# Attention heads in pairs with normalised weights, three expert tiles beside the ring, and one wait moved in a two-block transformer kernel

## The chip, the cores and the metric

The kernel runs on one core of one Trainium2 chip, as one program without a host in between. The metric is the device time of one execution in microseconds (us). The engines are called TensorE (PE in the rows; PEld is its weight load), VectorE (DVE), ScalarE (ACT), GpSimd (POOL) and SyncE (SP). SyncE here only issues transfers.

## What is computed

All numbers are 32-bit floats; the model width is 1024 and the sequence 256 rows. A first block of two layers works on the stream and on 256 context rows; a second block of two layers works on the first one's result and on 256 memory rows.

First block, per layer:

```python
hx = x * (1 + sc1) + sh1                     # modulation from c @ w_ada
q, k, v, cb, cc, cv, gu, gv = split(hx @ w_in)
att = window_attention(q, k, v, k_ctx, v_ctx, sink)    # 8 heads of 64, 2 key heads
o = concat([att, local_mixers(cb, cc, cv, gu, gv)]) @ w_out
x = layer_norm(ALPHA * x + g1 * o)
x = layer_norm(ALPHA * x + g2 * hier_moe(x * (1 + sc2) + sh2))   # 32 experts, top 2
```

In layer 0 the context rows go the same way, in layer 1 they give keys and values alone. Second block, per layer:

```python
ya = sliding_window_attention(rope(q_a), rope(k_a), v_a, sinks) * silu(g_a)   # 8 heads of 64
yb = forgetting_attention(q_b, k_b, v_b, log_sigmoid(f_b)) * silu(g_b)        # 8 heads of 64
yc = rms_norm(state_space_part * silu(z))
x = x + concat([ya, yb, yc]) @ w_out
x = x + memory_cross_attention(rms_norm(x), rms_norm(mem))                    # 4 heads of 256
```

In each of the attentions the weights of a row are p / (sum(p) + exp(sink - m)) with p = exp(s - m), where s are the masked scores and m their largest; those without a sink leave its term out.

## The kernel before

**Order.** Each engine has its program written out by hand, and they wait for each other by semaphores. The stages follow each other: layer 0 of the first block (projections, attention, mixing product, routing, experts), layer 1 the same, then the second block's layers.

**Ring.** All large weights come through a ring of four tiles of 2 MB. SyncE issues them in the order of use (`dense`, line 1278): for tile g it first waits until tile g - 4 is released, which the table `released` says as a semaphore and a count. The experts have three tiles each (w1, w3, w2), 96 in a layer, and TensorE takes them in that order from the ring; in a layer of 32 experts the first eleven tiles are written out and the rest run in loops (line 1315). The modulation weights (`ada`, line 584) pass through the ring too, and their products stand as filling work beside the attention.

**Attention.** A unit is one head of one tile of 128 query rows. `attention` exists three times, for TensorE (line 522), ScalarE (1524) and VectorE (1884). Per unit TensorE makes the scores (lines 568, 1120), VectorE adds mask and, in the forgetting attention, the sums of the gates, takes the row's maximum (1925) and writes its negative; ScalarE makes the exp with the row's sum beside it (1529); TensorE transposes the weights in blocks of 128 keys (507), ScalarE copies them out (1516), and TensorE weighs the values (541): the turned weights, 128x128, are the stationary operand, the values, 128x64, the moving one. Eight heads of a query tile share one bank. When they are done, VectorE asks ScalarE for the exp of the sinks, adds, takes the reciprocals and multiplies the bank by them (1899, 1833). The rows so attended are later transposed by TensorE and copied by ScalarE, since the product that follows wants the features on the partitions.

TensorE takes two units in turn; beside each unit a `fill` runs: products of the other projections, gate rows or modulation tiles in the first block, stream products in the second (1051 where the result is turned, 1037 where it is rows). VectorE takes the fills' results in `beside_first`, `beside_last`, `beside_a`, `beside_b`, ScalarE serves gelu, square root and other functions between its units, each with a change of its table. In layer 0 of the first block the products are fills 0 to 16 without every third, and the tiles of modulation rows 4 to 8 stand at fills 2, 5, 8, 11 and 14, rows 9 to 11 at 19, 21 and 23, and those of the next layer at 25, 27, 29 and 31. The tile of product weights that is released last, `cx_at`, is in use up to fill 16.

**Experts.** Tokens are gathered in blocks by GpSimd (line 1431) into `hb`, four blocks at a time, turned by TensorE (832), and each expert's three products run in 64-column halves side by side (866).

**Memory rows.** The second block's keys and values of the memory are made beside the first block. The last of them is written to `kv_scratch` by ScalarE's queue after the second layer's experts. VectorE waits for that transfer (`kv_out`, line 2548) ahead of the second block, since the buffer `hb` is written again there. The second block's first rows are taken in a loop over two row tiles (2655 to 2667).

```python
            def weigh(i):
                n, h = units[i]
...
                for k in range(nkc(n)):
                    last = mm(T["bank"][:, o:o + hw], sbuf_pT[:, i % 2, k, :], values(n, h, k),
                              start=(k == 0), stop=(k == nkc(n) - 1))
```

## Time and profile before

| | us |
|---|---|
| runs | 2308.99, 2307.2, 2302.45 |
| median | 2307.2 |
| the profiled execution | 2304.22 |
| its span, first to last instruction | 2302.4 |

The mean granted clock of TensorE in the profiled execution is 0.985. A row of the timeline gives start, duration, engine, line, operation, output and inputs, sizes, how many instructions are merged, and in brackets the idle time before it with what ended it. Durations of TensorE overlap their followers a little, since its ends are modelled. Busy shares are averages over stages with different limits, so the rows below are taken stage by stage.

### The profile page before, as it was taken

What the parts mean: (1) busy time and instruction counts of PE and PEld (TensorE: products, weight loads), DVE (VectorE), ACT (ScalarE), POOL (GpSimd) and SP (SyncE); (2) the same over time, 40 slices, a digit from 0 to 9 for tenths busy, and PEclk for the clock granted to TensorE, in tenths of its full rate; (3) what the DMA queues carried; (4) which work ended last, traced back from release to release, by engine and by line L of the source; (5) the groups of instructions that cost most, each with busy time, mean ns of one, the idle gap of its engine ahead of it and who ended that gap; (6) DMA issues with size and microseconds to landing.
All of it is one profiled execution on the core that took longest, in us unless ns stands there. A gap on an engine that the chain in (4) does not pass through costs nothing.

```text
span 2302.4 us, 30476 instructions
## 1 busy us (share of the span) xinstructions
PE 2035.6 (88%) x11971; PEld 1212.3 (53%) x11972; DVE 786.6 (34%) x1836; ACT 457.2 (20%) x1059; POOL 189.7 (8%) x240
## 2 busy tenths in 40 slices
PE   6999999799877789999877777798999999999998
PEld 4566566444433335757433333344875575775574
DVE  1355674111111116656111111114466312456413
ACT  2142112111111112411111111111123212123112
POOL 1000001111111110001111111111000000000000
PEclk9999999999999999999999999999999999999999
DMA  9235649999999985686999999996343332343230
GB/s 376 110 129 240 255 156 378 423 426 427 427 425 426 425 345 211 236 317 257 424 425 425 424 425 425 427 420 242 134 182 129 111 147 110 147 165 129 95 142 19
DMA packets 62872, 640.95 MB, mean 278 GB/s; under 512 B 15868, under 2 KB 16420, under 8 KB 24240
## 3 DMA queue, kind: packets, MB, share of 16 engines
q1 hardware_dynamic: 41728, 588.39, 61.9%
q0 software_dynamic: 19984, 44.74, 5.5%
q10 hardware_dynamic: 1056, 6.37, 0.7%
q8 instruction: 73, 1.20, 0.2%
q14 instruction: 31, 0.25, 0.0%
HBM read 622.50 MB, written 44.17 MB: 290 GB/s over the span
## 4 chain that ended last, share of the span: by engine, by line
PE 62%; DMA 31%; DVE 4%; ACT 2%; issue 1%; SPq 0%; POOL 0%; DVEq 0%
DMA ring<-in_moe 26%; PE ps L866 10%; PE ps L1037 10%; PE ps L519 8%; PE ps L1051 6%; PE ps L1148 5%; PE ps L507 3%; PE ps L695 3%; DMA ring<-in_denseA 3%; PE ps L1220 2%; PE ps L872 2%; PE ps L1016 2%; PE ps L541 2%; PE ps L771 2%; PE ps L584 1%; DMA ring<-in_denseB 1%
## 5 line engine op out<-in xcount | busy, mean ns | idle before, releaser
L866 PE MATMUL ps<-ring,scr 128*64 128x256 f32 (+1 forms) x4800 | 667.5, 430 | 178.2 <-DMA ring<-in_moe 169.3
L866 PEld LDWEIGHTS ps<-ring,scr 128*64 128x64 f32 x4800 | 333.4, 138 | 485.9 <-DMA ring<-in_moe 239.3
L1833 DVE TENSOR_TENSOR scr<-ps,scr 128x512 f32<-128x512 f32 (+3 forms) x98 | 54.6, 558 | 574.6 <-PE ps L866 487.0
L1037 PE MATMUL ps<-ring,hT 128*128 128x512 f32 (+1 forms) x576 | 245.5, 578 | 5.1 <-ACT hT L1546 5.1
L519 PE MATMUL ps<-ring,hT 128*128 128x512 f32 (+1 forms) x512 | 199.3, 547 | 0.5 <-ACT hT L1516 0.5
L1444 POOL DMA_INDIRECT ys_scratch<-scr,ytab x128 | 125.0, 976 | 825.4 <-DVE scr L2495 791.6
L1670 ACT ACTIVATE scr<-ps 128x512 f32<-128x512 f32 x64 | 38.2, 597 | 760.8 <-PE ps L866 694.0
L2495 DVE COPY scr<-ps 128x1024 f32<-128x1024 f32 x64 | 78.4, 1224 | 269.3 <-PE ps L866 243.4
L1037 PEld LDWEIGHTS ps<-ring,hT 128*128 128x128 f32 x576 | 108.1, 193 | 117.8 <-issue 108.2
L1516 ACT ACTIVATE scr<-ps 128x256 f32<-128x256 f32 (+2 forms) x168 | 71.3, 436 | 403.7 <-PE ps L507 403.7
L519 PEld LDWEIGHTS ps<-ring,hT 128*128 128x128 f32 x512 | 97.3, 193 | 93.0 <-issue 89.2
L1051 PE MATMUL ps<-hT,ring 128*128 128x256 f32 x640 | 145.5, 382 | 0.0
L1051 PEld LDWEIGHTS ps<-hT,ring 128*128 128x128 f32 x640 | 118.8, 190 | 17.4 <-issue 0.7
L1529 ACT ACTIVATE scr<-scr,small 128x256 f32<-128x256 f32 (+2 forms) x128 | 67.6, 528 | 50.0 <-DVE small L1837 40.9
L584 PE MATMUL ps<-ring,small 128*32 128x128 f32 x1536 | 55.9, 307 | 22.8 <-DMA ring<-in_denseA 22.8
L541 PEld LDWEIGHTS ps<-scr 128*128 128x128 f32 x512 | 66.0, 194 | 16.5 <-issue 15.3
L507 PE MATMUL ps<-cst,scr 128*128 128x128 f32 x332 | 61.1, 281 | 13.9 <-ACT scr L1529 11.6
L541 PE MATMUL ps<-scr 128*128 128x64 f32 x512 | 65.5, 274 | 2.7 <-DVE hb L1833 2.7
L695 PE MATMUL ps<-hT,ring 128*128 128x512 f32 (+1 forms) x192 | 65.6, 490 | 0.0
L584 PEld LDWEIGHTS ps<-ring,small 128*32 128x32 f32 x1536 | 47.7, 123 | 33.0 <-issue 16.4
L1833 DVE TENSOR_TENSOR scr<-ps,cst 128x256 f32<-128x256 f32 (+2 forms) x96 | 32.7, 341 | 85.5 <-PE ps L568 74.3
L872 PE MATMUL ps<-ring,scr 128*128 128x512 f32 x128 | 57.1, 599 | 5.0 <-DMA ring<-in_moe 5.0
(330 smaller groups left out, 2019.2 us busy)
## 6 DMA issues: line engine op xcount, KB each, us to landing
ring<-in_moe SPq DMA_DIRECT2D x192, 2048.0 KB, 15.9
ring<-in_denseB SPq DMA_DIRECT2D x48, 2048.0 KB, 7.7
ring<-in_denseA SPq DMA_DIRECT2D x36, 2048.0 KB, 16.2
scr<-ys_scratch POOLq DMA_DIRECT2D x6, 1024.0 KB, 7.2
modB<-mod_scratch POOLq DMA_DIRECT2D x10, 512.0 KB, 11.3
ring<-kv_scratch SPq DMA_DIRECT2D x2, 2048.0 KB, 8.6
tok_scratch<-hb POOLq DMA_DIRECT2D x6, 512.0 KB, 2.9
memT_scratch<-modB ACTq DMA_DIRECT2D x2, 1024.0 KB, 6.7
```

The lines of the kernel that those rows point to most:

```text
L507: last = nc.tensor.transpose(bank[:, i * P:(i + 1) * P], c, ident)
L519: last = mm(bank[:, 0:cols], lhs(c), w(c), start=(c == 0), stop=(c == n - 1))
L541: last = mm(T["bank"][:, o:o + hw], sbuf_pT[:, i % 2, k, :], values(n, h, k), start=(k == 0), stop=(k == nkc(n) - 1))
L584: last = mm(bank[32 * q:32 * q + 32, 0:P], cact32[:, c, :], w[:, c, q * P:(q + 1) * P], start=(c == 0), stop=(c == DC - 1))
L695: last = mm(T["open"][:, 0:tok], w[:, c, off:off + P], hT8[:, c, 0:tok], start=(c == 0), stop=(c == DC - 1))
L866: last = mm(out, lhs(c)[:, 0:64], w(c)[:, half * q:half * (q + 1)], start=(c == 0), stop=(c == n - 1))
L872: last = mm(ps[:, bank, :], lhs(c), w(c), start=(c == 0), stop=(c == n - 1))
L1037: last = mm(T["open"][:, 0:cols], hT16[:, c, t * P:(t + 1) * P], w[:, c, 0:cols], start=(c == 0), stop=(c == DC - 1))
L1051: last = mm(T["open"][:, q * 256:(q + 1) * 256], w[:, c, m * P:(m + 1) * P], hT16[:, c, :], start=(c == 0), stop=(c == DC - 1))
L1148: last = mm(bank, lhs(c), w[:, c, :], start=(c == 0), stop=(c == DC - 1))
L1444: pool.indirect_dma_start(halves, bass.IndirectOffsetOnAxis(ap=ytab[:, h, b:b + 1], axis=0), y[:, h * 512:(h + 1) * 512], None, bounds_che ...
L1833: return V.tensor_tensor(out, a, b, op)
```

## The change

**Pairs.** The five attentions with heads of 64 run as `paired_attention`; the memory attention keeps the old way under its own name. Units go two and two. The sink is one more column of the scores, so the row's sum holds it. VectorE takes the reciprocal per unit, ScalarE multiplies the weights by it, then they are transposed. In the weighing the values are stationary and the turned weights of 128 rows moving; the two heads of a pair use the two halves of the columns, so the result has its features on the partitions. The transpositions of the attended rows and their copies go; the gate streams `ga` and `gb` are made in turned form. The fills get new places.

**Tiles beside the ring.** In layer 1 the expert tiles at places 3, 7 and 10 of the order are loaded to buffers that are free there, in two halves each, and not through the ring; SyncE issues the first after the last query and key tiles are turned, the other two after the second expert tile. Blocks of tokens have two buffers there, where they had four.

**Wait.** VectorE's wait for `kv_out` moves from the end of the second layer's experts to the second row tile of the second block's first layer.

```diff
+ASIDE = ((), (3, 7, 10))
+
+BLOCK_BUFFERS = (4, 2)
...
-TURNED = ("x0", "x1", "x2", "qb", "kb")
+TURNED = ("x0", "x1", "x2", "qb", "kb", "ga", "gb")
...
+    own_beside = ((2, 5, 8, 11, 14, 16, 17, 19), (4, 6, 8, 9, 10, 11, 12, 13))
+    next_beside, product_beside = (22, 25, 28, 31), (0, 1, 2, 3, 5, 7)
...
+        def paired_attention(units, score, values, nkc, fill):
...
+            for i in range(0, len(units), 2):
+                n, h = units[i]
+                for k in (i, i + 1):
+                    need("scaled", p_scaled)
+                    turn_weights(k, nkc(n))
+                    turned = T["tp"]
+                    if k == i:
+                        for at in range(i + 2, min(i + 4, len(units))):
+                            score(*units[at])
+                    if k > 0:
+                        fill(k)
+                if h == 0:
+                    T["bank"] = av_bank()
+                pe.wait_ge(tp_free, turned)
+                for b in range(nkc(n)):
+                    for q in range(2):
+                        last = mm(T["bank"][HD * q:HD * q + HD, h // 2 * P:(h // 2 + 1) * P], values(n, h + q, b),
+                                  sbuf_pT[:, q, b, :], start=(b == 0), stop=(b == nkc(n) - 1))
...
-            for t in range(nt):
-                need("h", h_ready)
-                turn([hb[:, t, i * P:(i + 1) * P] for i in range(4)])
+            need("h", h_ready, nt)
...
-            for t in range(NX):
-                need("h", h_ready)
-                for c in (0, 4):
-                    turn([mixB[:, t, (c + i) * P:(c + i + 1) * P] for i in range(4)])
+            need("h", h_ready)
+            out_attended(0, 0)
+            need("h", h_ready)
...
+            if l > 0:
+                sp_.wait_ge(*free_when["turned", l])
+                load_aside(0)
+            expert_tile(0)
+            expert_tile(1)
+            if l > 0:
+                sp_.wait_ge(*free_when["routed", l])
+                sp_.wait_ge(rows_out, 16 * 9)
+                load_aside(1)
+                load_aside(2)
...
+        def paired_attention(units, nkc, sink, serve, after=None):
+
+            for i in range(0, len(units), 2):
+                for k in (i, i + 1):
+                    n, h = units[k]
+                    weights(k, n, h, P * nkc(n) + sink)
+                for k in (i, i + 1):
+                    n, h = units[k]
+                    p = sbuf_p[:, k % 2, 0:P * nkc(n)]
+                    T["inv"] += 1
+                    act.wait_ge(inv_ready, T["inv"])
+                    A(p, p, ACT.Copy, scale=rinv[:, n, h:h + 1]).then_inc(p_scaled, 1)
+                for k in (i, i + 1):
+                    copy_turned(sbuf_pT[:, k % 2, 0:nkc(units[k][0]), :], nkc(units[k][0]))
+                    if after:
+                        after(k)
+                if i > 0:
+                    serve(i - 1)
+                serve(i)
+            serve(len(units) - 1)
...
+            for i in range(0, len(units), 2):
+                for k in (i, i + 1):
+                    scores(k)
+                if i == 0 and opening:
+                    opening()
+                for k in (i, i + 1):
+                    inverse(k)
+                if i > 0:
+                    extra(i - 1)
+                extra(i)
+                if i > 0 and units[i][1] == 0:
+                    finish(units[i][0] - 1, av_job())
...
-                dve.wait_ge(kv_out, 16 * 2 * DEPTH)
...
+                if l == 0 and t == 1:
+
+                    dve.wait_ge(kv_out, 16 * 2 * DEPTH)
```

## Rows read from the trace of the kernel before

**Rows 1.** The page: busy time and share of each engine; the chain that ended last.

```profile
PE 2035.6 (88%) x11971; PEld 1212.3 (53%) x11972; DVE 786.6 (34%) x1836; ACT 457.2 (20%) x1059; POOL 189.7 (8%) x240
...
PE 62%; DMA 31%; DVE 4%; ACT 2%; issue 1%; SPq 0%; POOL 0%; DVEq 0%
DMA ring<-in_moe 26%; PE ps L866 10%; PE ps L1037 10%; PE ps L519 8%; PE ps L1051 6%; PE ps L1148 5%; PE ps L507 3%; PE ps L695 3%; DMA ring<-in_denseA 3%; PE ps L1220 2%; PE ps L872 2%; PE ps L1016 2%; PE ps L541 2%; PE ps L771 2%; PE ps L584 1%; DMA ring<-in_denseB 1%
```

**Rows 2.** Stretches: length, busy time per engine, clock, DMA share, GB/s.

```profile
1040.00:1080.00 40.00, 36.24 (x200) 30.06 (x199) 26.32 (x109) 7.13 (x13) 4.92 (x6) 0.96 0.55 194
1080.00:1160.00 80.00, 65.48 (x505) 35.23 (x506) 16.78 (x36) 14.77 (x30) 11.56 (x13) 1.00 1.01 425
...
1730.00:1750.00 20.00, 20.00 (x74) 10.48 (x72) 19.02 (x52) 5.28 (x15) 0.00 (x0) 1.00 0.27 105
1600.00:1610.00 10.00, 8.21 (x21) 5.68 (x22) 6.44 (x22) 2.98 (x10) 0.00 (x0) 0.66 0.11 23
```

**Rows 3.** TensorE in order of time, first block's attention, four key chunks.

```profile
122.27 1.90 PE L541 MATMUL ps<-scr 128*128 128x64 f32 x16
...
125.59 1.95 PE L584 MATMUL ps<-ring,small 128*32 128x128 f32 x64
```

**Rows 4.** TensorE in order of time, second block's forgetting attention: one chunk, two chunks.

```profile
1722.87 0.55 PE L541 MATMUL ps<-scr 128*128 128x64 f32 x4
...
1739.72 1.00 PE L541 MATMUL ps<-scr 128*128 128x64 f32 x8
```

**Rows 5.** TensorE in order of time, second layer's experts.

```profile
1093.11 1.09 PE L832 MATMUL ps<-cst,hb 128*128 128x128 f32 x8
1094.13 3.65 PE L866 MATMUL ps<-ring,scr 128*64 128x512 f32 x16
...
1111.30 3.67 PE L866 MATMUL ps<-ring,scr 128*64 128x256 f32 x32 [1.32 <-DMA ring<-in_moe]
```

**Rows 6.** ScalarE in order of time, first block's attention: copy, exp.

```profile
133.78 0.60 ACT L1516 ACTIVATE scr<-ps 128x512 f32<-128x512 f32 x1 [4.31 <-PE ps L507]
134.27 0.71 ACT L1529 ACTIVATE scr<-scr,small 128x512 f32<-128x512 f32 x1
```

**Rows 7.** Line 1529: its table loads, ns shortest/median/longest, first and last start.

```profile
L1529 ACT ACT_TABLE_LOAD  x10: 1283/1283/1283, 111.7 to 2238.1; - x10
```

**Rows 8.** TensorE in order of time, end of layer 0's attention.

```profile
203.60 3.64 PE L584 MATMUL ps<-ring,small 128*32 128x128 f32 x64 [1.89 <-DMA ring<-in_denseA]
...
240.17 1.73 PE L541 MATMUL ps<-scr 128*128 128x64 f32 x8
...
247.25 2.31 PE L519 MATMUL ps<-ring,hT 128*128 128x512 f32 x5
```

**Rows 9.** SyncE's queue in order of time, 194 to 212 us.

```profile
195.91 11.72 SPq L1278 DMA_DIRECT2D ring<-in_denseA  x5
```

**Rows 10.** VectorE in order of time: layer 1's first norm; start of the second block.

```profile
1017.32 1.23 DVE L1841 SCALAR_TENSOR_TENSOR hb<-modB,scr 128x1024 f32<-128x1024 f32 x1 [4.57 <-DMA scr<-in_ln_b]
...
1599.16 0.09 DVE L2654 MEMSET scr<- 128x36 f32 x1 [11.52 <-DMA kv_scratch<-hb]
```

**Rows 11.** TensorE in order of time, start of the second block.

```profile
1585.01 3.94 PE L1037 MATMUL ps<-ring,hT 128*128 128x280 f32 x16
...
1589.66 7.03 PE L1037 MATMUL ps<-ring,hT 128*128 128x512 f32 x16
1601.79 13.39 PE L1037 MATMUL ps<-ring,hT 128*128 128x280 f32 x32 [5.10 <-ACT hT L1546]
```

**Rows 12.** TensorE in order of time: between the second block's attentions, and their end.

```profile
1701.61 0.49 PE L1120 MATMUL ps<-scr 64*128 64x128 f32 x2 [0.43 <-DVE scr L1841]
1702.97 0.33 PE L507 MATMUL ps<-cst,scr 128*128 128x128 f32 x1 [0.87 <-ACT scr L1529]
...
1784.52 1.04 PE L507 MATMUL ps<-cst,hb 128*128 128x128 f32 x8
...
1787.70 2.84 PE L1148 MATMUL ps<-ring,scr 128*128 128x512 f32 x6 [0.74 <-ACT scr L1516]
```

446 lines of the change are left out of this document (230 added, 216 removed).

## The prediction

> **What bounds the kernel now.** I read the page's shares and its chain first [rows 1]: TensorE is busy for 88% of the span and holds 62% of the chain that ended last, DMA 31%, and 26% of the span is expert weights arriving in the ring. VectorE and ScalarE together hold 6%. So two prices are paid: TensorE work in the dense stages, and bytes in the expert stages. The stretches show it [rows 2]: from 1080 to 1160 us the queues move 425 GB/s at a full DMA share and TensorE is busy 65.48 of 80 us, waiting for tiles as at 1111.30 [rows 5]; from 1040 to 1080, ahead of the second layer's experts, they move only 194; from 1730 to 1750, in the second block's attention, TensorE is busy all 20 us and VectorE 19.02 of them. An edit that shortens TensorE work counts in the last kind of stretch, one that takes bytes out of the ring in the first, and in the attention the next engine to be late is VectorE.
>
> **Part 1: the pairs.** Five attentions run 56 pairs of units: 8 of four key chunks and 8 of two in the first block's layer 0, 8 of four in layer 1, and per layer of the second block 8 of one chunk and 8 of two.
>
> *Weighing.* A four-chunk pair holds 1.90 us of TensorE (16 records) [rows 3], a two-chunk pair 1.00 and a one-chunk pair 0.55 [rows 4]. After the change the values stand still in 64 columns, and two heads stream 128 columns each into the two halves. The trace has that form at other widths: an expert product of 32 records in 128x64 halves, 256 columns each, takes 3.67 us [rows 5], so 16 records of 128 columns are 3.67/4 = 0.92; a modulation product, 64 records of 128 columns in four groups, takes 1.95 [rows 3], so 16 in two groups are 1.95 x 16/64 x 2 = 0.98. I take half of the old time less the overlapped ends: a gain of about 0.8, 0.35 and 0.15 us per pair. The other bound is the old durations, no gain.
>
> The rows show no price for changing the form: a 128x128 transposition of 1.09 us starts at 1093.11 and the 128x64 product at 1094.13, before the first one's modelled end [rows 5]. The Trainium skill (TensorEngine Tiling (Array Packing), Tiling Modes) says that a change of tiling mode drains the engine, and TensorE: Matmul & The Clock Gate puts a drain at some 175 ns. By that, two changes for each of 56 pairs would give back 112 x 0.175 = 19.6 us, an estimate from those pages; the row speaks against it, since it has no gap between the modes.
>
> *The longer chain.* Before, a unit went exp, transposition, copy, weighing, and the division came later, eight heads at once. Now exp (0.71 for 512 columns [rows 6]) is followed by VectorE's reciprocal and by a ScalarE scaling, as large as a copy (0.60 [rows 6]), before TensorE may transpose. Scores run one pair ahead, so this hides behind two fills where those are products of some 3.6 us; it shows where a fill is missing or something else sits in ScalarE's order. The sink column costs VectorE a short copy per unit, and the two reciprocals wait for exps that follow the pair's second score work. Queued behind them on VectorE are the takes of the fills.
>
> *Second block, per layer.* In the window attention 4 one-chunk pairs x 0.15 + 4 two-chunk x 0.35 = 2.0 us, on TensorE's path. Between it and the forgetting attention TensorE stood still for 0.43 + 0.87 us [rows 12]; the closing of the first now comes behind the opening of the second, so I count 1.3. The forgetting attention would give 2.0 again, but VectorE is at 95% there [rows 2]: with two reciprocals and a wait for the second exp, about 1 us per pair by the exp's duration, its pairs outlast TensorE's for three or four pairs, and I count 1.3. The 16 transpositions of the attended rows ended the stage: from 1784.52 to the output product at 1787.70, 3.2 us [rows 12], go. The turned gate streams cost about 0.2 (estimate, two short transposed products for two of rows). Sum 2.0 + 1.3 + 1.3 + 3.2 - 0.2 = 7.6 per layer, **-15.2 us** for both. Bounds: -6, if only the transpositions stay gained, to -22.
>
> *Layer 0 of the first block.* The first eight pairs gain 8 x 0.8 = 6.4. Against that the first pair waits for its whole chain, some 2.2 (two exps and a scaling, rows 6), and the gelu's and the square root's table changes, 1.28 there and 1.28 back each [rows 7], now stand in front of a pair's scalings with one product to cover them: some 4.5. So the last product ends where it did, +0.3. There its tile comes free, SyncE's next issues follow at 195.91 [rows 9], and the tile behind them is used at 203.60 [rows 8]. Before, that was in fill 19 of 31; now it is fill 16, and everything later stands behind the same landing. From there to the end of weighing (240.17 + 1.73) lay 38.3 us [rows 8] for 6.5 pairs, (38.3 - 3.6)/6.5 = 5.3 each without the first product; one more pair lies behind it now: +5.3. The 6.5 others gain 0.35 each and pay about 0.8 each for a scaling and two hand-overs that their short fills do not hide: +2.9. The attended rows' transpositions go: from the last weighing to the mixing product at 247.25 lie 5.3 us [rows 8], of which about 1 stays: -4.3. Sum 0.3 + 5.3 + 2.9 - 4.3 = **+4 us**. Bounds -2 (the chain hides as well as before) to +8.
>
> *Layer 1 of the first block.* The same 6.4, and half of the transpositions, 2.1, less about 5.5 for the start, the gelu and the square root, would bring the mixing product 3 us earlier. But what follows does not hang on TensorE alone: VectorE waits for `scr<-in_ln_b` until 1017.32, 4.57 us idle [rows 10], a transfer that POOL issues behind its modulation rows, and the extra expert tile that is loaded in this attention competes with it. I take **+1 us**, from -3 (those transfers move forward too) to +4.
>
> **Part 2: three tiles beside the ring.** A tile is 2.097 MB and at 425 GB/s [rows 2] takes 4.93 us. Three less in the ring's stream are 14.8 us, if they are loaded in time that is free: the 40 us before run at 194 GB/s [rows 2], which leaves 40 x 231 GB/s = 9.2 MB, more than 6.3. What it adds: SyncE waits at two places ahead of later tiles, none of which had a free slot there, and on POOL's queue the last two of four gathers of tokens wait for the first two blocks to be turned, with the loads of the closing norm behind them. The third block is wanted only at 1093.11 [rows 5], more than 10 us after. Behind an aside tile no slot comes free, so the queues may run empty for up to 2 us: **-13 us**, bounds -6 (TensorE's starting pace is the limit) to -15.
>
> **Part 3: the moved wait.** VectorE stands 11.52 us for `kv_scratch<-hb` until 1599.16 [rows 10], ahead of the first norm. TensorE stands 5.10 us and from 1601.79 runs 32 records in 13.39 us, where the same records took 3.94 + 7.03 = 10.97 just before [rows 11]; the granted clock in 1600 to 1610 is 0.66 [rows 2], between the levels of 1.2 and 2.4 GHz. With the wait at the second row tile, TensorE goes on from 1596.7 with those 32 records, which cover the landing. If the standstill goes, so do 5.10 + 2.42 = **-7.5 us**. Bounds -5 to -8: the products behind those records need VectorE's second tile, and each us by which the landing outlasts them costs one.
>
> **Sum.** -15.2 + 4 + 1 - 13 - 7.5 = -30.7 us on the profiled execution's 2304.2: 2273.5. The median of the runs shown, 2307.2, stands 3.0 above it, so I predict **2276 us**.
>
> **Rivals.** (a) The second block's pairs wait for VectorE throughout: for it speak the 19.02 of 20 us, against it that the convolution's work, which fills VectorE there, stands beside 8 of the forgetting attention's 16 units and 4 of the window attention's. The gain falls from 15.2 to about 2: 2289. (b) The tiles beside the ring give 5 us, as slots come free at TensorE's pace: 2284. (c) Weighing in halves keeps its old duration, by a drain or because the halves do not overlap: 6.4 + 2.8 + 6.4 + 4 x 2.0 = 24 us lost, 2300; rows 5 speak against it. (d) Slower: the first block's 24 pairs each show their chain of exp, reciprocal and scaling ahead of the transposition. At 2 us more per pair (two exps and a scaling, rows 6) that is 48: 2324. It decides from 30.7/24 = 1.28 us per pair. Against it: the products that stand beside most pairs. (e) The first block's stands hide after all and its pairs keep their gain, 13 us more: 2263. The change does what it says as far as the diff shows.
>
> **Chances.** Forecast 0.55, (a) 0.13, (b) 0.10, (c) 0.04, (d) 0.08, (e) 0.10. A measurement of this kernel can tell about 0.3%, 7 us, from no change. Faster by more: the forecast, (a), (b) and (e) less their bad ends, 0.86; within it those ends and (c), 0.06; slower (d), 0.08. The range 2257 to 2298 takes in (a), (b), (e) and the bounds of the costs together, and leaves out (c) and (d).
>
> **What would show it.** Right: weighing of a four-chunk pair under 1.1 us; no transpositions between the last weighing and the output products; the second expert stage shorter by about 13 us; no stand of TensorE near 1600. Wrong: TensorE waiting for ScalarE or VectorE in every pair of the second block; idle queues between 1080 and 1130; a mixing product of layer 0 over 10 us later.

## The result and the profile after

The changed kernel takes 2293.98 us (median of 7 runs, 2291.82 to 2297.82) against 2307.2 (2302.45 to 2311.1) for the kernel before, measured beside it: a ratio of 0.9947 with an interval of 0.9936 to 0.9958. That is 13.2 us faster where 31 were forecast; the time lies inside the range given, the gain at 42% of its size. In the profiled executions the spans are 2292.2 and 2302.4 us, 10.2 apart.

The page of the kernel after, its busy times and its chain, answers to [rows 1]:

```profile
PE 2013.8 (88%) x12043; PEld 1196.0 (52%) x12044; DVE 796.0 (35%) x1984; ACT 500.6 (22%) x1147; POOL 189.7 (8%) x240
...
PE 56%; DMA 29%; DVE 9%; ACT 3%; issue 1%; SPq 0%; POOL 0%; DVEq 0%
```

TensorE has 22 us less to do, and the span gains less than half of that. On the chain TensorE and DMA shrink, and VectorE goes from 4 to 9% and ScalarE from 2 to 3%: new waits stand where work was taken out.

To see where, I cut the span at the start of TensorE's first row of each stage (first score product, first mixing product, first expert product, first product of the memory's keys and values, first window score of the second block, first state-space product). The stretches between, in us; the runs e1 to e12 are told below:

| stretch | before | after | e1 | e2 | e3 | e8 | e10 | e12 |
|---|---|---|---|---|---|---|---|---|
| layer 0: attention to mixing | 135.5 | 146.7 | 136.8 | 150.5 | 135.4 | 136.2 | 136.1 | 135.2 |
| layer 0: mixing to experts | 108.8 | 110.4 | 110.5 | 110.0 | 111.9 | 108.5 | 112.7 | 111.8 |
| layer 1: attention to experts | 153.6 | 156.7 | 157.0 | 152.6 | 156.1 | 154.7 | 152.9 | 154.5 |
| layer 1: experts | 479.5 | 469.3 | 468.5 | 480.5 | 469.0 | - | 472.4 | 469.8 |
| memory rows to second block's first scores | 70.5 | 62.9 | 67.2 | 62.9 | 63.0 | 63.0 | 62.9 | 62.6 |
| second block, layer 0: both attentions and output product | 169.3 | 164.9 | 165.0 | 165.0 | 165.0 | 163.0 | 164.9 | 165.0 |
| the same, layer 1 | 169.3 | 165.0 | 165.4 | 165.1 | 165.7 | 163.0 | 165.2 | 165.2 |

After against before: layer 0's attention +11.2 and the 0.3 by which it begins later, its mixing product +1.6, layer 1 +3.1, experts -10.2, moved wait -7.6, second block -4.4 and -4.3; the sum is the span's -10.2 (to 0.1, the rounding). Every term of the forecast moved its way, but layer 0's attention loses 11 us where 4 were counted, and the second block gives 8.7 where 15.2 were. The mixing product of layer 0 starts 11.5 us later (258.75 against 247.25), which the prediction had named as a sign of being wrong.

**Layer 0's attention.** TensorE in order of time, kernel after, answering to [rows 8]:

```profile
205.20 3.23 PE L619 MATMUL ps<-ring,small 128*32 128x128 f32 x64 [7.61 <-DMA ring<-in_denseA]
...
224.47 0.44 PE L531 MATMUL ps<-cst,scr 128*128 128x128 f32 x2 [2.58 <-ACT scr L1604]
...
253.61 0.66 PE L574 MATMUL ps<-scr 128*64 128x128 f32 x8
256.19 0.63 PE L531 MATMUL ps<-cst,hb 128*128 128x128 f32 x4 [1.93 <-DVE small L2328]
```

The last product ends and releases its tile, and TensorE stands 7.61 us for the modulation tile that now follows at once. All eight two-chunk pairs are weighed behind it. Two more such stands follow (1.29 and 1.96 us), and between 220 and 252 TensorE stands nine times for ScalarE's copies (line 1578) and scalings (line 1604), 8.0 us in all.

**Weighing.** The first window attention of the second block, a pair of one chunk. First the kernel after (fill, weighing, transposition, scores), further down a pair of two chunks (with the transposition ahead of its fill) and, from the first block, one of four:

```profile
1628.58 3.62 PE L1091 MATMUL ps<-hT,ring 128*128 128x256 f32 x16
1632.13 0.44 PE L574 MATMUL ps<-scr 128*64 128x128 f32 x4
1632.50 0.33 PE L531 MATMUL ps<-cst,scr 128*128 128x128 f32 x1
1632.75 0.49 PE L603 MATMUL ps<-scr 64*128 64x128 f32 x4
...
1672.52 0.38 PE L531 MATMUL ps<-cst,scr 128*128 128x128 f32 x2
...
1676.27 0.66 PE L574 MATMUL ps<-scr 128*64 128x128 f32 x8
1676.86 0.44 PE L531 MATMUL ps<-cst,scr 128*128 128x128 f32 x2
...
144.91 1.09 PE L574 MATMUL ps<-scr 128*64 128x128 f32 x16
145.93 0.66 PE L531 MATMUL ps<-cst,scr 128*128 128x128 f32 x4
```

The same of the kernel before:

```profile
1630.51 3.62 PE L1051 MATMUL ps<-hT,ring 128*128 128x256 f32 x16
1633.96 0.55 PE L541 MATMUL ps<-scr 128*128 128x64 f32 x4
1634.35 0.28 PE L507 MATMUL ps<-cst,scr 128*128 128x128 f32 x1
1634.56 0.51 PE L568 MATMUL ps<-scr 64*128 64x128 f32 x4
...
1678.10 1.00 PE L541 MATMUL ps<-scr 128*128 128x64 f32 x8
1678.94 0.39 PE L507 MATMUL ps<-cst,scr 128*128 128x128 f32 x2
...
122.27 1.90 PE L541 MATMUL ps<-scr 128*128 128x64 f32 x16
124.00 0.60 PE L507 MATMUL ps<-cst,scr 128*128 128x128 f32 x4
```

Read from start to start, not by the durations. Weighing: four chunks 1.73 before, 1.02 after; two chunks 0.84 and 0.59; one chunk 0.39 and 0.37. And the neighbours grow: the same fill ahead of the weighing takes 3.45 before and 3.55 after, the transposition behind it 0.21 and 0.25. So a one-chunk pair loses 0.12 us, a two-chunk pair gains 0.11 and a four-chunk pair, if its neighbours grow as much, 0.6.

**The end of that stage.** Kernel after, answering to the last of [rows 12]: stream products run straight into the output product, and no transposition of attended rows stands between.

```profile
1775.44 6.60 PE L1077 MATMUL ps<-ring,hT 128*128 128x512 f32 x15
1781.88 7.03 PE L1189 MATMUL ps<-ring,hb 128*128 128x512 f32 x16
```

**The experts of layer 1.** The queues during that stage: the total, then the ring's queue and GpSimd's. Kernel before (1075.3 to 1554.9 us):

```profile
DMA packets 18990, 203.36 MB, mean 424 GB/s; under 512 B 5881, under 2 KB 5881, under 8 KB 6635
...
q1 hardware_dynamic: 13590, 198.01, 97.5%
q0 software_dynamic: 5242, 4.11, 2.6%
```

Kernel after (1091.7 to 1561):

```profile
DMA packets 18832, 198.07 MB, mean 422 GB/s; under 512 B 5854, under 2 KB 5854, under 8 KB 6864
...
q1 hardware_dynamic: 13156, 191.70, 96.8%
q0 software_dynamic: 5520, 5.16, 3.2%
```

The ring brings 6.3 MB less, which is three tiles. But GpSimd's queue brings 1.05 MB more inside the stage: with two block buffers in place of four, two of the four gathers come later, when the queues are full. GpSimd in the kernel before (the last of the four) and in the kernel after (the third; the fourth follows at 1098.32):

```profile
1062.38 0.94 POOL L1431 DMA_INDIRECT hb<-tok_scratch,slot_tok  x1 [0.30 <-issue]
```

```profile
1090.74 0.93 POOL L1493 DMA_INDIRECT hb<-tok_scratch,slot_tok  x1 [13.40 <-PE ps L865]
```

The stage saves 5.29 MB, not 6.29. It also begins less evenly: a stretch of the kernel after ahead of it (columns as in [rows 2]):

```profile
1080.00:1091.00 11.00, 9.57 (x48) 8.01 (x46) 4.97 (x21) 2.07 (x5) 0.26 (x1) 1.00 0.24 63
```

The queues run at 63 GB/s there; then the stage's first 32 records, at 1091.66, take 5.36 us at a granted clock of 0.68, where they take 3.67 at the full clock [rows 5].

**Layer 1's first norm.** VectorE in the kernel after, answering to the first of [rows 10], where it stood 4.57 us for the same transfer and the row began 16.5 us earlier:

```profile
1033.81 1.22 DVE L1916 SCALAR_TENSOR_TENSOR scr<-modB,scr 128x1024 f32<-128x1024 f32 x1 [9.41 <-DMA scr<-in_ln_b]
```

The attention begins 13.25 us later here, so 3.2 us are lost inside this layer; VectorE waits longer, for a transfer.

**The moved wait.** TensorE in the kernel after, answering to [rows 11]: no stand between 1591 and 1613.

```profile
1591.33 3.94 PE L1077 MATMUL ps<-ring,hT 128*128 128x280 f32 x16
1595.10 1.04 PE L531 MATMUL ps<-cst,S 128*128 128x128 f32 x8
1595.97 17.67 PE L1077 MATMUL ps<-ring,hT 128*128 128x512 f32 x48
```

### The profile page after: what moved, and what is told of

Same layout as the page of the kernel before. It is cut to its first block, busy times and chain, and to the rows that moved or that the text cites. A ratio compares the mean times of both kernels' runs of the same rounds, so it can differ in the third digit from the quotient of the medians.

```text
span 2292.2 us, 30890 instructions
## 1 busy us (share of the span) xinstructions
PE 2013.8 (88%) x12043; PEld 1196.0 (52%) x12044; DVE 796.0 (35%) x1984; ACT 500.6 (22%) x1147; POOL 189.7 (8%) x240
## 4 chain that ended last, share of the span: by engine, by line
PE 56%; DMA 29%; DVE 9%; ACT 3%; issue 1%; SPq 0%; POOL 0%; DVEq 0%
DMA ring<-in_moe 25%; PE ps L899 11%; PE ps L543 8%; PE ps L1077 8%; PE ps L1091 5%; PE ps L1189 5%; PE ps L531 3%; PE ps L1259 2%; PE ps L905 2%; PE ps L1056 2%; PE ps L803 2%; DVE scr L1908 2%; DMA ring<-in_denseA 2%; DVE scr L1916 1%; DMA ring<-in_denseB 1%; PE ps L731 1%
## 5 line engine op out<-in xcount | busy, mean ns | idle before, releaser
L899 PE MATMUL ps<-ring,scr 128*64 128x256 f32 (+1 forms) x4736 | 653.6, 428 | 172.5 <-DMA ring<-in_moe 163.9
L899 PEld LDWEIGHTS ps<-ring,scr 128*64 128x64 f32 x4736 | 328.4, 138 | 472.2 <-DMA ring<-in_moe 229.3
L1091 PE MATMUL ps<-hT,ring 128*128 128x256 f32 x896 | 204.1, 382 | 0.0
L1077 PE MATMUL ps<-ring,hT 128*128 128x512 f32 (+1 forms) x448 | 184.6, 566 | 0.0
L1091 PEld LDWEIGHTS ps<-hT,ring 128*128 128x128 f32 x896 | 166.2, 190 | 26.0 <-issue 3.3
L543 PE MATMUL ps<-ring,hT 128*128 128x512 f32 (+1 forms) x416 | 157.2, 531 | 0.2 <-issue 0.2
L1077 PEld LDWEIGHTS ps<-ring,hT 128*128 128x128 f32 x448 | 83.5, 190 | 85.6 <-issue 82.8
L543 PEld LDWEIGHTS ps<-ring,hT 128*128 128x128 f32 x416 | 78.6, 191 | 70.3 <-issue 67.3
L1590 ACT ACTIVATE scr<-scr,small 128x513 f32<-128x513 f32 (+4 forms) x128 | 67.8, 531 | 70.8 <-DVE small L1912 48.6
L531 PEld LDWEIGHTS ps<-cst,scr 128*128 128x128 f32 x332 | 38.2, 142 | 60.4 <-ACT scr L1604 29.7
L803 PE MATMUL ps<-scr,ring 128*128 128x256 f32 x256 | 64.7, 415 | 0.0
L1967 DVE TENSOR_REDUCE small<-scr 128x1 f32<-128x256 f32 (+2 forms) x128 | 58.0, 453 | 6.8 <-DVE scr L1908 0.3
```

Source lines behind the costliest of these rows:

```text
L531: last = nc.tensor.transpose(bank[:, i * P:(i + 1) * P], c, ident)
L543: last = mm(bank[:, 0:cols], lhs(c), w(c), start=(c == 0), stop=(c == n - 1))
L803: last = mm(T["open"][:, q * 256:(q + 1) * 256], w[:, c, m * P:(m + 1) * P], memT[:, c, :], start=(c == 0), stop=(c == DC - 1))
L899: last = mm(out, lhs(c)[:, 0:64], w(c)[:, half * q:half * (q + 1)], start=(c == 0), stop=(c == n - 1))
L1077: last = mm(T["open"][:, 0:cols], hT16[:, c, t * P:(t + 1) * P], w[:, c, 0:cols], start=(c == 0), stop=(c == DC - 1))
L1091: last = mm(T["open"][:, q * 256:(q + 1) * 256], w[:, c, m * P:(m + 1) * P], hT16[:, c, :], start=(c == 0), stop=(c == DC - 1))
```

## The experiments

Each run changes the kernel after unless it says otherwise. Ratios are to the kernel before on the same chip, whose medians lay between 2304.1 and 2305.9 us. Executions of one kernel spread over 3 to 10 us here, and a stage may differ by 3 to 4 us between two kernels with the same code in it: layer 1 below, and layer 0's attention, which takes 146.7 us in the kernel after, 150.5 in e2 and 151.1 in e7, with granted clocks of 0.83, 0.74 and 0.74 from 225 to 245 us. Smaller differences are read only where a stage is steadier: the experts of layer 1 take 467.5 to 469.3 us in the eight traces with three tiles beside the ring, the second block 164.9 to 165.7 per layer wherever its code is that of the change.

**e1: the first block with the old attention.** TensorE's, ScalarE's and VectorE's parts of the first block, its fills and its closing as before; the second block, the tiles and the wait as after.

```diff
-            paired_attention([(n, h) for n in range(nt) for h in range(NH)],
+            attention([(n, h) for n in range(nt) for h in range(NH)],
...
-                    if i in own_beside[0]:
-                        ada(own_at[4 + own_beside[0].index(i)])
...
+                    elif i in (19, 21, 23):
+                        ada(own_at[9 + (i - 19) // 2])
```

> The first block's two attentions go back to their old form (heads normalised at the end, rows turned afterwards, modulation tiles at fills 19, 21, 23 and 25 to 31); second block, tiles beside the ring and the moved wait stay as changed. Theory 1 (the first block's pairs are what gives the gain back): the mixing product of layer 0 starts again near 247 us (258.75 in the changed kernel, 247.25 before), layer 0's experts near 356 (369.20), and the total falls by 13.2 us for layer 0 and by up to 3 for layer 1's start of the experts: 2278 to 2281 us. Rival (the loss lies in what else changed in the first block: the residual's buffer, the tiles beside the ring, their transfers): layer 0's experts stay within 3 us of 369 and the total within 4 us of 2294.

Measured: 2286.74 us, ratio 0.9917 (0.9903 to 0.9932), so 7 faster than the kernel after, between the two theories. Layer 0's attention is back at 136.8. The pairs of the first block, as the change places them, cost time. The other theory's time is missed in part because the stretch ahead of the second block takes 67.2 us in this trace and not 62.9; e4 below shows why.

**e2: no tiles beside the ring, four block buffers.**

```diff
-ASIDE = ((), (3, 7, 10))
-BLOCK_BUFFERS = (4, 2)
+ASIDE = ((), ())
+BLOCK_BUFFERS = (4, 4)
```

> The changed kernel with all 96 expert tiles of layer 1 in the ring again and four buffers for the gathered blocks. Theory: the second expert stage is longer by the 10.3 us that it lost (79.5 us per 16 tiles as before), and the first of its products starts as late after the mixing product as in the changed kernel (77.0 us; 73.3 before), because VectorE's modulation rows come later, not because the tiles' transfers compete: total 2304. Rival (the first extra tile's transfer delays the modulation rows and the norm's parameters): the distance from mixing product to first expert product returns to 73.3 us, total 2301.

Measured: 2303.71 us, ratio 0.9996 (0.9985 to 1.0008): 10 us slower than after, and the experts' stage back at 480.5. The first expert product comes 72.5 us after the mixing product, the rival's distance (73.3) and not the theory's (77.0); but e7, with the tiles and the same code, has 75.0, so this does not decide whether the tiles' transfers compete. The tiles give 10 to 11 us, and without them the whole rest of the change, moved wait included, comes out at no change.

**e3: layer 0's modulation tiles at the fills of the kernel before.**

```diff
-    own_beside = ((2, 5, 8, 11, 14, 16, 17, 19), (4, 6, 8, 9, 10, 11, 12, 13))
-    next_beside, product_beside = (22, 25, 28, 31), (0, 1, 2, 3, 5, 7)
+    own_beside = ((2, 5, 8, 11, 14, 19, 21, 23), (4, 6, 8, 9, 10, 11, 12, 13))
+    next_beside, product_beside = (25, 27, 29, 31), (0, 1, 2, 3, 5, 7)
```

> The changed kernel with layer 0's modulation tiles at their old fills: own ones at 19, 21, 23, next layer's at 25, 27, 29, 31. Theory 1 (the tile used directly behind the release of the last product's tile makes TensorE stand 7.6 us, and one pair more lies behind that landing): the mixing product of layer 0 starts 4 to 7 us earlier than 258.75, near 253, total 2287 to 2290. Rival (the two-chunk pairs are bound by the chain of score work, exp, reciprocal, scaling, turning, wherever the tiles stand): not more than 2 us earlier, total 2292 to 2294.

Measured: 2278.02 us, ratio 0.9879 (0.9862 to 0.9895): 16 us faster than after, by two lists of numbers. Layer 0's attention takes 135.4 us. TensorE in order of time, e3:

```profile
198.72 0.66 PE L574 MATMUL ps<-scr 128*64 128x128 f32 x8 [0.57 <-ACT scr L1578]
...
205.49 3.64 PE L619 MATMUL ps<-ring,small 128*32 128x128 f32 x64 [4.04 <-DMA ring<-in_denseA]
...
242.17 0.66 PE L574 MATMUL ps<-scr 128*64 128x128 f32 x8
```

The tile lands as late as in the kernel after (205.49 and 205.20). But one pair has been weighed before it, at 198.72, and half of the next one's work is done, since the tile is the second fill of its pair (19) and not the first (16). So 6.5 pairs stand behind the landing, not 8; the stand is 4.04, and from the landing to the end of the last weighing go 37.3 us, not 49.1. Without the first product that is (37.3 - 3.6)/6.5 = 5.2 us per pair, against (49.1 - 3.2)/8 = 5.7. In the old places each of the last seven pairs has one modulation tile beside it. In the new ones the first two tiles share a pair, and two pairs (fills 20 and 21, 26 and 27) have none and show their chain.

**e4: the moved wait alone, in the kernel before.**

```diff
-                dve.wait_ge(kv_out, 16 * 2 * DEPTH)
...
+                if l == 0 and t == 1:
+                    dve.wait_ge(kv_out, 16 * 2 * DEPTH)
```

> The kernel before with the wait for the memory rows moved alone. Theory: the stand of 5.10 us near 1600 goes and the records behind it run at full clock, 7.9 us as in the changed kernel: 2299.3. Rival (in the kernel before the landing at 1599 would now stop the second tile's rows instead): under 4 us, above 2303.

Measured: 2300.66 us (10 runs) against 2304.91, ratio 0.9983 (0.9972 to 0.9994), -4.3 us. In its stage the stand at 1601 is gone: the 48 records there and what follows up to the next kind of product take 17.5 us (1592.29 to 1609.80), as in the kernel after, where they took 25.4 (1589.66 to 1615.02). But a stand 20 us earlier, 1.54 us in the kernel before, is longer, and the clock falls behind it (0.83 granted from 1578 to 1588). VectorE, then TensorE, e4:

```profile
1567.81 0.75 DVE L1837 TENSOR_SCALAR scr<-scr,gates 128x1024 f32<-128x1024 f32 x1 [12.78 <-DMA scr<-ys_scratch]
...
1575.60 2.48 DVE L1833 TENSOR_TENSOR S<-S,lnB 128x1024 f32<-128x1024 f32 x2
```

```profile
1578.18 1.24 PE L507 MATMUL ps<-cst,S 128*128 128x128 f32 x8 [3.09 <-issue]
1579.21 8.60 PE L1016 MATMUL ps<-ring,hb 128*128 128x512 f32 x16
```

The same in the kernel before:

```profile
1577.24 1.06 PE L507 MATMUL ps<-cst,S 128*128 128x128 f32 x8 [1.54 <-issue]
```

TensorE turns the rows of `S` 0.1 us after VectorE's norm has written them (1575.60 + 2.48 here; in the kernel before at 1577.13), and VectorE's norm waits for the load of the experts' results, `scr<-ys_scratch`: 11.24 us in the kernel before, 12.78 here. So the stretch fell from 70.5 to 65.9 and not to the kernel after's 62.9, by 1.5 us of a later landing and 1.6 of the lower clock. In e1 the same stand is 3.26 us behind a wait of 12.99, and the 16 records after it take 9.00 us. Besides, the second block's layer 0 takes 171.0 us in e4 and not 169.3, at a granted clock of 0.95 to 0.96 from 1680 to 1720. Why the load lands later in these two traces stays open.

**e5: the old rhythm in layer 1 too**, on top of e3.

```diff
-    ... (4, 6, 8, 9, 10, 11, 12, 13)
-    product_beside = (0, 1, 2, 3, 5, 7)
+    ... (2, 4, 6, 8, 10, 11, 12, 13)
+    product_beside = (0, 1, 3, 5, 7, 9)
```

> As e3, with layer 1's fills at their old places too: products at 0, 1, 3, 5, 7, 9, own modulation tiles at 2, 4, 6, 8 and 10 to 13. Theory (layer 1's start of the experts is set by the chain of modulation rows that POOL spreads and the norm's parameters behind them, and the new order makes those rows 2 to 3 us later): VectorE's wait for the parameters ends 2 to 3 us nearer to the start of that attention, the distance from its first score to the first expert product falls from 156.1 us (e3) to 153 to 154, total 2275 to 2276. Rival (the longer chain of the pairs sets it, the mixing product comes no earlier): distance within 1 us of 156, total 2278.

Measured: 2287.03 us, ratio 0.9918 (0.9903 to 0.9933), 9 slower than e3; layer 1 from attention to experts takes 160.7. The theory that the fills cost layer 1 something as well fell: there the new places are the better ones.

**e6: layer 1's gates taken before the attention is closed**, on top of e3.

```diff
+            if l > 0:
+                for t in range(nt):
+                    take_gates(t)
...
-            else:
-                for t in range(nt):
-                    take_gates(t)
```

> As e3, but in layer 1 VectorE takes the gate rows (2.52 us) before it closes the last heads, in the 3.0 us in which it waits for TensorE's last weighing. Theory: the mixing product starts 2.5 us earlier, since TensorE's stand of 3.84 us ahead of the gates' turning goes, but the first expert product does not move (under 0.5 us), because VectorE waits for the norm's parameters anyway; total 2278. Rival (TensorE's end of the attention binds): the first expert product comes 2.5 us earlier, total 2275.

Measured: 2279.56 us, ratio 0.9893 (0.9875 to 0.9911), the same as e3. The mixing product came 75.5 us after the first score in place of 80.0, yet what follows it grew from 76.1 to 77.7 us. GpSimd in e6:

```profile
1001.40 0.60 POOL L1416 DMA_DIRECT2D mod_scratch<-scr  x1
1016.32 0.55 POOL L1416 DMA_DIRECT2D scr<-in_ln_g  x1 [14.31 <-DMA mod_scratch<-scr]
```

The norm's rows are asked for only when the modulation rows have landed, 14 us after their issue, and VectorE waits 12.56 us for them, where the kernel after has 9.41. That queue, and not the attention, sets when layer 1's norm may begin. The two stretches together are 2.9 us shorter in e6's profile, and the medians do not show it.

**e7: one more product of 128 columns beside each fill of the second block**, in halves (128x64) in its layer 0 and in the full form (128x128) in layer 1. What it writes is overwritten by the weighing.

```diff
+                    if probe and h > 0:
+                        mm(T["bank"][0:probe, h // 2 * P:(h // 2 + 1) * P], cst[:, 0:probe], cst[:, 0:P],
+                           start=True, stop=True)
```

> The changed kernel with one more TensorE product of constants ahead of each fill of three of four pairs in the second block (its result is overwritten): in layer 0 in the form 128x64, in layer 1 in the form 128x128, 128 columns each. Theory (a change of form costs TensorE some 0.07 us each way beyond the product): in layer 0 the step from the transposition to the fill grows by 0.25 to 0.3 us per product, in layer 1 by 0.11 to 0.15. Rival (no price for the form): both grow by the same 0.1 to 0.15.

Measured: 2306.99 us (one execution); the second block's stretches are 175.3 (halves) and 169.3 (full form), against 165.0. For 24 products each, 10.3/24 = 0.43 us apiece in halves and 4.3/24 = 0.18 in the full form. TensorE in order of time, layer 0 and then layer 1 (transposition, extra product, fill, and the weighing that follows):

```profile
1673.95 0.38 PE L531 MATMUL ps<-cst,scr 128*128 128x128 f32 x2
1674.26 0.43 PE L568 MATMUL ps<-cst 128*64 128x128 f32 x2
1674.62 3.70 PE L1080 MATMUL ps<-ring,hT 128*128 128x512 f32 x8
1678.25 0.66 PE L577 MATMUL ps<-scr 128*64 128x128 f32 x8
...
2029.94 0.38 PE L531 MATMUL ps<-cst,scr 128*128 128x128 f32 x2
2030.16 0.39 PE L568 MATMUL ps<-cst 128*128 128x128 f32 x2
2030.38 3.60 PE L1080 MATMUL ps<-ring,hT 128*128 128x512 f32 x8
2033.91 0.66 PE L577 MATMUL ps<-scr 128*64 128x128 f32 x8
```

The same transposition takes 0.31 us ahead of a product in halves and 0.22 ahead of one in the full form; the product itself 0.36 and 0.22; the fill behind it 3.63 and 3.53. From the transposition to the weighing go 4.30 and 3.97 us, and 3.75 in the kernel after (1672.52 to 1676.27): the product costs 0.55 us in halves and 0.22 in full form, and the 0.33 between them is the price of two changes of form, some 0.16 each. The means over 24 are lower for halves because 10 of the 24 stand behind scores, whose own form (64 rows, 64x128) changes there anyway: a full-form product takes 0.33 us behind them and not 0.22. So the halves add 14 x 2 + 10 = 38 changes, and the 6.0 us between the two layers are again 0.16 each. The theory's direction held, its price of 0.07 was less than half of it.

**e8: no scaling of the weights.** The normalisation is left out, so the rows that reach the router differ, the tokens go to other experts, and times from layer 0's experts to those of layer 1 are not compared.

```diff
-                for k in (i, i + 1):
-                    n, h = units[k]
-                    p = sbuf_p[:, k % 2, 0:P * nkc(n)]
-                    T["inv"] += 1
-                    act.wait_ge(inv_ready, T["inv"])
-                    A(p, p, ACT.Copy, scale=rinv[:, n, h:h + 1]).then_inc(p_scaled, 1)
...
-                    need("scaled", p_scaled)
+                    need("p", p_ready)
```

> The changed kernel without the normalisation: TensorE turns the weights as soon as the exp is there, ScalarE's scalings are left out. Theory (the chain shows only where fills are short or ScalarE changes tables, so in the first block and not in the second): the first block's attentions get shorter, layer 0's by 3 to 5 us and layer 1's by 4 to 6, the second block's by under 2 us per layer. Rival (the chain is what takes the second block's gain): 3 us or more per layer there.

Measured: layer 0's attention 136.2 (after: 146.7), layer 1's up to the mixing product 75.4 (79.6), the second block 163.0 per layer (164.9). TensorE, e8: the tile lands at 199.53, where after has 205.20.

```profile
199.53 3.64 PE L618 MATMUL ps<-ring,small 128*32 128x128 f32 x64 [7.79 <-DMA ring<-in_denseA]
...
240.64 0.66 PE L573 MATMUL ps<-scr 128*64 128x128 f32 x8
```

The stand of some 7.7 us is the same: it belongs to the place. But it comes 5.7 us earlier, since the pairs ahead are faster, and the last weighing 13 us earlier.

**e9: the first of the three tiles loaded with the other two**, on top of e3.

```diff
-                load_aside(0)
...
-                load_aside(1)
-                load_aside(2)
+                for n in range(3):
+                    load_aside(n)
```

> As e3, but the first of the three extra expert tiles is issued with the other two, after the routing, and no longer during layer 1's attention. Theory (its 2 MB compete with the modulation rows and the norm's parameters, on which VectorE waits): the distance from layer 1's first score to its first expert product falls from 156.1 us (e3) to about 153, as without the extra tiles (152.6 in e2), and the experts' stage stays 469 us long, since there is room on the queues until 1080: total 2275. Rival (no competition; the two executions of the same code already differ by 3 us here, 156.6 and 153.3): distance and total as in e3, 2278, or worse by the queues' fuller time before the experts.

Measured: 2277.32 us, ratio 0.9883 (0.9866 to 0.9899), not told apart from e3. From the first score to the first expert product go 152.0 us, as the theory had it; since the same code with the early tile gave 152.9 (e10) to 156.7 (after), that does not decide it.

**e10: two tiles beside the ring, two block buffers**, on top of e3.

```diff
-ASIDE = ((), (3, 7, 10))
+ASIDE = ((), (3, 7))
...
-                load_aside(2)
```

> As e3 with two tiles beside the ring (places 3 and 7) and not three. Theory (with all slots full the queues stand idle from the last load until TensorE gives back the first slot, a loss of some 4.6 us that does not depend on how many tiles lie beside): the experts' stage is longer than e3's 469.0 us by one tile's 4.95, 474. Rival (each tile beside the ring is worth a third of the 10.3 us, 3.4): 472.4.

Measured: 2284.89 us (one execution); the experts' stage 472.4, which is the rival's number. So the third tile brings 3.4 us (469.0 in e3), and no fixed loss by idle queues eats it.

**e11: e6 and e9 together.**

> e6 and e9 together: gate rows taken before the last heads are closed, the first extra tile issued late. Theory (with the parameters' wait shortened, the earlier mixing product counts): the distance from first score to first expert product is 151 to 152 us, total 2273. Rival: as e9.

Measured: 2277.55 us, ratio 0.9886 (0.987 to 0.9903). Neither edit adds to e3.

**e12: two tiles beside the ring with four block buffers**, on top of e9.

```diff
-ASIDE = ((), (3, 7, 10))
-BLOCK_BUFFERS = (4, 2)
+ASIDE = ((), (7, 10))
+BLOCK_BUFFERS = (4, 4)
```

> As e9 with two tiles beside the ring (places 7 and 10, in buffers that need none of the token rows) and four buffers for the gathered blocks as before the change. Theory (with two buffers the third and fourth gather, 0.5 MB each, are read inside the stage that is bound by the queues, 1.05 MB / 425 GB/s = 2.5 us, and that is what three tiles lose of 14.8 us): the experts' stage is 479.5 - 2 x 4.93 = 469.6 us, as long as with three tiles and two buffers (467.5 to 469.3) and 2.5 us shorter than e10's 472.4; total 2277 to 2279. Rival (each tile is worth 3.4 to 3.75 us, as slots stay empty behind it): 472 or more, total 2281.

Measured: 2282.43 us, ratio 0.9897 (0.9879 to 0.9915); the stage 469.8, that is 9.7 below the kernel before's 479.5: two tiles at 4.93 us each are 9.9. With two buffers two tiles gave 7.1 (e10). The difference is 2.6, where the late gathers work out at 1.05 MB by 424 GB/s, 2.5 us; e9's edit, which e12 has as well, may have up to 1.0 of it (the stage is 468.0 in e9 and 469.0 in e3), and e12 keeps other tiles aside (places 7 and 10, not 3 and 7). It is one trace each, and eight traces of one stage lie 1.8 apart. The time as a whole, 2282.43, is nearer to the rival's 2281 than to the theory's 2277 to 2279; the stage is what bears on the theory.

The best kernel is the change with layer 0's modulation tiles where they were: e3, e9 and e11, 2277.3 to 2278.0 us, 27 us below the kernel before.

## Why the prediction was right and wrong

**The moved wait: right.** -7.5 forecast, -7.6 in the profile. The 32 records behind the standstill cover the landing, and the lower clock went with the stand. Alone it gave 4.3 by the medians (e4): in e4's trace the place itself is 7.9 us shorter, but a later load ahead of it and two stretches at a lower clock take 4.9 back.

**The tiles beside the ring: right in kind, 3 us too high.** -13 forecast, -10.2 measured, within its bounds. The term missed was in the change's own text: two block buffers for four. The prediction looked at whether the gathers would be late for TensorE, and they are not; it did not count that their bytes now fall into a stage that is bound by bytes. Three tiles are 14.8 us, less 2.5 for the gathers, is 12.3; the remaining 2.1 is the mean rate of 422 in place of 424 GB/s over the whole stage (198.07 MB at either rate: 2.2 us). Of it the stage's first 60 us have 1.0 (412, 425 and 408 GB/s in steps of 20, against 420, 424 and 423 before), and a dip near the end has the rest (392 and 370 GB/s from 1500 to 1520, against 406 and 408 at about the same products before). That the gathers cost time is seen in their bytes and in e10 against e12; this division is worked out, not tested by a run.

**The second block: -8.7, not -15.2. The step that failed is "the rows show no price for changing the form".** I read a product that starts before the modelled end of the transposition ahead of it as proof that no time lies between. In these rows the modelled ends of such small products overlap their followers in either form; the row to compare it with is the same transposition ahead of a product of its own form. That row, kernel before, with the first product of [rows 11] that follows at 1589.66:

```profile
1588.78 1.04 PE L507 MATMUL ps<-cst,S 128*128 128x128 f32 x8
```

Start to start, the eight of [rows 5] take 1.02 us ahead of a product in halves (1093.11 to 1094.13), these eight 0.88 ahead of one in the full form. The price was in the trace: 0.14. In e7 it is 0.16 per change.

The Trainium skill (TensorEngine Tiling (Array Packing), Tiling Modes) says that changing the tiling mode drains the engine; the traces here agree, with 0.14 to 0.16 us per change. The same page (When to Use Tiling) advises, for 64 moving columns, the very exchange of operands that this change makes; here the weighing of four chunks falls from 1.73 to 1.02 us, and that of one chunk gains nothing. The Trainium skill (Perfetto Trace Analysis, Tensor Engine Instruction (MATMUL, LD_WEIGHTS)) also says that TensorE's ends in a profile are estimated from the instruction's size, which is the trap above.

By terms, per layer: the window attention was to give 2.0, and by the milestones of its pairs gave 0.9; the forgetting attention with the boundary was to give 2.6 and gave 0.3, the boundary 1.5 and its pairs -1.2 (short stands for the scaling, 0.16 to 0.47 each, such as 0.47 at 1756.20); the transpositions at the end were to give 3.2 and gave 3.2. So what is gained in the second block is mostly the transpositions, as the lower bound of -6 had it. The weighing was to give 2.0 in each attention, and by the pairs above it gives nothing: four lose 0.12, four gain 0.11, and two changes of form per pair, 0.28 to 0.32 us, are more than the 0.24 to 0.27 by which each missed. Of the window attention's 0.9, two short waits that are gone have 0.7 (0.33 at 1630.34 in the kernel before; the scores at 1669.91 took 1.00 and now take 0.63). A second part is the scaling: in e8 the forgetting attention up to the output product takes 86.1 us, not 88.0, while the window attention stays at 70.05. So the scaling costs 1.9 per layer, where the prediction had allowed 0.7. Rival (a), that the pairs wait for VectorE throughout, would have left a gain of 2 us; 8.7 are left, and e8, which takes the whole scaling out of the chain, gains only 2.0 per layer. Rival (c) was the nearest: a part of it, the price of the form, is what happened, though not the whole old duration.

**Layer 0 of the first block: +11.5, not +4. The steps that failed are "one more pair lies behind it now: +5.3" and "-4.3" for the transpositions.** The place and the cause were right: the tile behind the last release is used at fill 16, at 205.20, and TensorE stands for it. The terms in order: up to the landing +1.6 for +0.3; from the landing to the end of the last weighing 49.1 us for 38.3, so +10.8 for 5.3 + 2.9 = 8.2; from there to the mixing product -0.9 for -4.3.

The middle term was short by half a pair. Fill 19 was the second of its pair and fill 16 is the first, so 8 pairs stand behind the landing where 6.5 did, one and a half more. The price of a pair was right: (5.3 x 7.5 + 2.9)/7.5 = 5.7 forecast, (49.1 - 3.2)/8 = 5.7 measured. In it are nine stands for ScalarE, 8.0 us, and two more for the ring, 3.25. Neither the longer chain nor the places alone cost the 11 us: e3 keeps the chain and e8 keeps the places, and each is 10 to 11 us faster. In e3 1.5 pairs go back in front of the landing, which at 5.2 each are 7.8 us of the 11.7 between the two, and a pair falls from 5.7 to 5.2, which makes up the other 4; in e8 the eight pairs fall to (41.8 - 3.6)/8 = 4.8, and the landing comes 5.7 us earlier. This division is worked out; no run moves the late tile alone or gives the two empty pairs a tile alone.

The last term, -4.3 for the transpositions between attention and mixing, came out at -0.9: from the last weighing's end to the mixing product are 5.35 us before [rows 8] and 258.75 - 254.27 = 4.5 after. Where they stood, TensorE now waits for VectorE's closing (1.93 at 256.19) and turns the gates. And in the old places (e3) the pairs bring layer 0 nothing: 135.4 against 135.5.

**Layer 1 of the first block: +3.1 in the profile, +1 forecast, not settled.** The same code there gave 153.3 in e7 and 152.9 in e10, and 152.6 without the tiles (e2). That is within the spread between executions. That the norm's transfers on GpSimd's queue decide and not TensorE, as the prediction had it, e6 shows.

**What the sum missed.** Forecast -30.7, profile -10.2. Of the 20.5, the second block has 6.5 (the price of the form, and the scaling beyond what was allowed for it), layer 0 7.5 up to its mixing product and 1.6 behind it, which no term covered, layer 1 2.1, the tiles 2.8. Layer 0's part depends on where the tiles stand: e3 has it back. Its 2278.0 us, 27 below the kernel before, is near the 2276 forecast by luck, since the second block gives 6.5 less there too. The stated range has a slip: the upper bounds of the terms, -6 + 8 + 4 - 6 - 5, together give 2302, not 2298; and two exps and a scaling are 2.0 us by [rows 6], not 2.2. Neither changes the account.

That the pairs of the first block (e3) beat the old attention there (e1) is not shown. Their medians lie 8.7 us apart and their profiles 3.6, because e3's profiled execution is its slowest, 6.4 above its median, and e1's is 1.2 above. The largest difference of a stage is the 4.2 in the stretch ahead of the second block, which is the same late load as in e4 and not the attention; layer 0's attention is 1.4 shorter.

## What to carry to other kernels

Take the length of a short product from its start to the next start, ahead of a follower of the same and of another form; the difference is what a change of form costs, and small products that change it twice must save more than twice that. When filling work is moved, count to the half pair what then stands behind the place where the ring's next tile is released late. When a chain between engines grows, look at each turn for the work that covers it. A buffer taken to hold something else moves transfers: count their bytes in the stage into which they move.

## What the runs showed of the hardware that was not expected

A change between products in full form and in halves of 64 columns costs TensorE 0.14 to 0.16 us, before and after alike; a product of 128 columns put between products in full form costs 0.55 us in halves and 0.22 in full form (e7).

The queues reach 422 to 424 GB/s as a mean over 470 us even with gathers among the ring's tiles, so that 1 MB more in such a stage is worth some 2.5 us (e10 against e12: 2.6).

A load that lands a little later can cost twice. For the same load VectorE waits 11.24 us in the kernel before, 11.59 after, 12.78 in e4 and 12.99 in e1; TensorE behind it stands 1.54, 1.77, 3.09 and 3.26 us. Behind the two short stands the next 16 records take 7.03 us at the full clock, behind the two long ones 8.60 and 9.00, with a granted clock of 0.83 in e4 from 1578 to 1588 and 0.66 in e1 from 1570 to 1580.
